# Minus the biased attention score and its minimum from one VectorE operation per branch, with the score scale moved into the key norm's weights

## The chip, the cores and the metric

The kernel runs on one core of a Trainium2 chip. The metric is the device time of one execution in microseconds (us). Three runs of the kernel before took 1355.65, 1356.13 and 1357.22 us; the median is 1356.13 us.

## What is computed

The reference is a trunk of two decoder layers over 256 tokens of width 1024. Each layer projects the normed input once, feeds three groups of heads (a state space model, a convolution module and a sparse attention), adds them through an output projection, and goes on with cross attention and a feed-forward part (dense in layer 0, the best two of eight experts in layer 1). The change lies in the sparse attention, of which these lines matter:

```
q = rms_norm(q, q_gain)                                  # 8 query heads of 64
k_slc = rms_norm(k_s, k_gain[1]);  k_win = rms_norm(k_w, k_gain[2])   # 2 key heads each
scale = HEAD_DIM ** -0.5
s_s = einsum(q, k_slc) * scale + bias_s                  # bias: table[bucket(distance)], masked where the key is later
s_w = einsum(q, k_win) * scale + bias_w
p = exp(s - max(s)) / sum(exp(s - max(s)))               # per row, for each branch by itself
o = gate_s * (p_s @ v_s) + gate_w * (p_w @ v_w) + gate_c * (compressed branch)
```

With 256 tokens every block is selected and the window covers all keys, so the selected and the window branch (below: b = 0 and b = 1) have the same bias and the same mask and differ in their keys and values.

## The kernel before

The 256 queries are two blocks (i = 0, 1) of 128 rows, which lie on the 128 partitions. Block 0 sees 128 keys, block 1 sees 256 (nk). A loop of 16 steps v runs over block and head, v = 8 i + n, in each layer; the code of each engine has this loop and its order is written out by hand. Every engine works through its own queue in order and waits on semaphores. The counter u is 20 l + v.

What each engine does at step v:

- TensorE, function scores(p), line 1837: one product for both branches of a head, into PSUM bank 0 (even v) or 1 (odd v), for the pair of heads v = 2p and 2p + 1. scores(p) is issued at the end of step v = 2p - 3, after the transposes and values of that step. The second bank of a pair may be written when VectorE has drained step 2p - 1, so the scores run one pair ahead of the softmax. banks.open is that wait.
- VectorE, lines 1330 to 1340: waits for the product and for the s_of buffer, forms scale times score plus bias of both branches in one operation (line 1337, 128 x 2 nk elements, PSUM and SBUF into SBUF) and adds one to the bank's drain semaphore; it waits for that itself, then takes the negated row maximum of both branches in one operation (line 1340) and adds one to max_ready. M holds the bias rows, read backwards.
- ScalarE, function probs, line 577: waits for max_ready, then one exponential per branch with the row maximum as its bias and the row sum as a second output (the read of the accumulator is a record of its own). After the second it adds one to probs_ready. Then it copies the transposed probabilities of step v - 1 out of PSUM (pt_copy, line 585).
- TensorE: waits for probs_ready, transposes the probabilities (line 1902), and multiplies those of step v - 1 with the values (function values, line 1572).

Other work is placed between these steps: on VectorE after step 1 the inner part of the compression, the centring of the convolution's layer norm and the gate of the state space model (lines 1191 to 1215), after step 2 the sums of the compressed keys (lines 1090, 1224), after step 5 and 13 the scores of the compressed branch (lines 1275 to 1282), after step 6 gate_halves (line 1295), after step 9 combine (lines 1300 to 1312) and the gain of the convolution's norm (line 1257), after step 10 conv_silu (line 1264). On TensorE fillers (line 1924, products that nobody reads) stand ahead of scores(p).

gk holds the products of the query and key gains, one column per layer and branch; it is made once at the start (lines 1115 to 1120). Its columns 1 and 2 multiply the keys of the two branches when they are copied to kT (line 1185), column 0 multiplies the compressed keys, whose scores are scaled by themselves at line 1275.

Of the kernel before, what the change touches and what calls it, by code (L numbers as in the profile page):

```python
# [19 lines left out]
ALU = mybir.AluOpType  # L20
ACT = mybir.ActivationFunctionType
AX = mybir.AxisListType.X

P = 128
# [18 lines left out]
SCALE = HD ** -0.5  # L43
# [199 lines left out]
def trunk(nc, x, mem, w_in, w_small, w_x, w_out, t5_table, ffn_w, router, moe_w, par_cols, s5_lam, s5_bc,  # L243
          consts, t5_hot, bias_rows, out):
    with ExitStack() as ctx:
        sem = Sems(nc, ctx)
        banks = Banks(sem)
# [10 lines left out]
        def ps(name):  # L258
            return pb[banks.bank(name)]
# [9 lines left out]
        M = late[0][:, 0:NH * FX].rearrange("p (h x) -> p h x", h=NH)  # L269
        par = sb("par", [P, 268])  # L270
        gk = sb("gk", [P, L, 4])
# [34 lines left out]
        nmx = sb("nmx", [P, 4, 2])  # L306
        sums = sb("sums", [P, NT, 2, NH])
# [47 lines left out]
        s_of = [scr[:, 0], scr[:, 1], spare[:, 0], spare[:, 1]]  # L355
        pt_of = [scr[:, 2], scr[:, 3], spare[:, 2], spare[:, 3]]

        def at(v): return (v + 2) % 4
# [13 lines left out]
        G_TAPS, G_HEAD = P, P + 64 * L  # L372
# [15 lines left out]
        for l in range(L):  # L388
# [3 lines left out]
            for c in range(CH if l == 0 else 0):  # L392
                s = FF_SLOTS[c]
# [125 lines left out]
        def _(act):  # L519
# [55 lines left out]
            def probs(buf, b, src, scale, to, m):  # L575

                return act.activation(s_of[buf][:, b * src.shape[-1]:(b + 1) * src.shape[-1]], src, ACT.Exp,  # L577
                                      bias=nmx[:, m, b:b + 1], scale=scale, accum_out=to)
# [12 lines left out]
            for l in range(L):  # L591
# [142 lines left out]
                for v in range(2 * NH + 1):  # L734
# [2 lines left out]
                    nk = P * (i + 1)  # L737
                    u = 20 * l + v
                    if v < 2 * NH:
                        act.wait_ge(sem["max_ready"], u + 1)  # L740
                        for b in range(2):
                            e = probs(at(v), b, s_of[at(v)][:, b * nk:b * nk + nk], 1.0, sums[:, i, b, hh:hh + 1], at(v))
                        e.then_inc(sem["probs_ready"], 1)
                    if v == 1:
                        cmp_tanh()
# [196 lines left out]
        def _(dve):  # L942
            n_own = [0]

            def own(i):
                n_own[0] += 1
                i.then_inc(sem["dve_step"], 1)
                dve.wait_ge(sem["dve_step"], n_own[0])
# [149 lines left out]
            for l in range(L):  # L1098
# [12 lines left out]
                if l == 0:  # L1111
                    for make in (weights, s5_turns(0)):
                        for _ in make:
                            pass
                    for m in range(L):
                        for b in range(3):
                            own(dve.tensor_tensor(gk[:, m, b:b + 1], par[:, G_HEAD + m:G_HEAD + m + 1],
                                                  par[:, G_HEAD + 2 + 3 * m + b:G_HEAD + 3 + 3 * m + b], ALU.mult))
                        own(dve.tensor_tensor(gk[:, m, 3:4], par[:, G_HEAD + 8 + m:G_HEAD + 9 + m],
                                              par[:, G_HEAD + 10 + m:G_HEAD + 11 + m], ALU.mult))  # L1120

# [202 lines left out]
                for v in range(2 * NH):  # L1324
                    i, n = divmod(v, NH)
                    hh = HEADS[n]
                    nk = P * (i + 1)
                    u = 20 * l + v
                    nm = f"sc{i}{n}_{l}"
                    banks.wait(dve, nm)  # L1330
                    if v >= 4:
                        banks.wait(dve, transposed(u - 4))
                    elif u >= 2 and v < 2:
                        banks.wait(dve, transposed(u - 2))
                    bias = M[:, hh, P:P * i + 256][:, ::-1].unsqueeze(1).to_broadcast([P, 2, nk])
                    S = s_of[at(v)][:, 0:2 * nk].rearrange("p (b s) -> p b s", b=2)
                    dve.scalar_tensor_tensor(S, ps(nm)[:, 0:2 * nk].rearrange("p (b s) -> p b s", b=2), SCALE, bias,
                                             ALU.mult, ALU.add).then_inc(banks.drain(nm), 1)
                    dve.wait_ge(banks.drain(nm), banks.count(nm, None, False) + 1)
                    dve.tensor_reduce(nmx[:, at(v)], S, AX, ALU.max, negate=True).then_inc(sem["max_ready"], 1)  # L1340
                    if v == 1:
                        cmp_inner()
                        ln_center()
                        glu_out()
                        cmp_gated()
                    if v == 2:
                        cmp_sums()
                    if v == 3:
                        cmp_keys()
                    if v == 4:  # L1350
                        cmp_keys_in()
                    if v == 5:
                        ln_scale()
                    if v == 6:
                        gate_halves()
                    if v in C_EXPS:
                        c_scores(C_EXPS.index(v))
                    if v in C_SUMS:
                        c_sums(C_SUMS.index(v))
                    if v == COMBINE:  # L1360
                        combine(0)
                    if v == CONV_GAIN:
                        conv_gained()
                    if v == CONV_SILU:
                        conv_silu()
                    if v == Y_SCALE:
                        y_scale(0)
# [879 lines left out]
```

## Time and profile before

| | us |
|---|---|
| median of three runs | 1356.13 |
| lowest, highest run | 1355.65, 1357.22 |
| span of the profiled execution, first to last instruction | 1354.2 |
| the same execution's time outside the span | not recorded; median less span is 1.9 |
| TensorE busy in the span | 1301.9 |
| VectorE busy in the span | 636.3 |
| ScalarE busy in the span | 424.7 |
| line 1337, 32 operations | 17.6 |
| line 1340, 32 operations | 17.7 |

The attention loop of layer 0 lies at 98 to 150 us of the span and that of layer 1 at 548 to 601 us. Times in the rows below count from the start of the span. In the timeline rows a group "x4" is four instructions of one kind that follow each other; for TensorE the first number is the start of the first of them and the second the time from there to the modelled end of the last. A bracket gives the idle time of that engine ahead of the row and what ended it. Layer 1's loop shows the same pattern as layer 0's, 449.8 us later at its start and 451.0 us later at its end.

### The profile page before, as it was taken

The numbers are of one execution on the slowest core, as the hardware profiler recorded it, in microseconds if no ns is written. First come the engines' busy times: TensorE is split into PE (matmuls) and PEld (weight loads), VectorE is DVE, ScalarE is ACT, GpSimd is POOL, SyncE is SP. The second block draws the span as 40 slices with busy tenths as digits, with TensorE's granted clock in tenths as the row PEclk, the third lists the DMA queues.
The fourth block names the chain that finished last, engine by engine and source line by source line (L and its number), as shares of the span: only waits on it lengthen the run. The fifth ranks groups of instructions, "written<-read, shape, count | busy, mean of one in ns | idle before, by whom it ended". The sixth has DMA issues, their size and how long they took to land.

```text
span 1354.2 us, 48384 instructions
## 1 busy us (share of the span) xinstructions
PE 1301.9 (96%) x21480; PEld 1076.0 (79%) x21480; DVE 636.3 (47%) x1404; ACT 424.7 (31%) x847; POOL 89.6 (7%) x139
## 2 busy tenths in 40 slices
PE   6999898999999999989889999999999999999998
PEld 5756555777777685654679999999999999999997
DVE  7877313013321246751345555555545555555554
ACT  4426313001002131541323334343343433334342
POOL 0350100000000027000000000000000000000000
PEclk8999999999999999989999999999999999999999
DMA  8530044224331154102669999999999999999990
GB/s 353 216 124 3 1 186 191 92 106 186 152 128 62 69 208 156 64 1 99 274 225 423 426 426 427 426 426 426 427 426 426 427 425 428 425 426 426 426 391 33
DMA packets 32865, 357.68 MB, mean 264 GB/s; under 512 B 3715, under 2 KB 5379, under 8 KB 6700
## 3 DMA queue, kind: packets, MB, share of 16 engines
q1 hardware_dynamic: 30656, 353.78, 63.2%
q10 hardware_dynamic: 2156, 3.18, 0.7%
q8 instruction: 35, 0.57, 0.2%
q14 instruction: 18, 0.15, 0.0%
HBM read 355.88 MB, written 1.06 MB: 264 GB/s over the span
## 4 chain that ended last, share of the span: by engine, by line
PE 89%; DVE 5%; ACT 2%; issue 2%; POOL 1%; DMA 1%; POOLq 0%; DVEq 0%; SPq 0%; ACTq 0%
PE bank L2109 29%; PE bank L1564 27%; PE bank L2125 14%; PE bank L2056 6%; PE bank L2171 2%; PE bank L1572 2%; PE bank L2096 2%; PE bank L1837 1%; PE bank L1714 1%; PE bank L1584 1%; PE bank L1902 1%; PE bank L1924 1%; DVE ring L970 1%; ACT ring L536 1%; PE bank L1658 1%
## 5 line engine op out<-in xcount | busy, mean ns | idle before, releaser
L2109 PE MATMUL bank<-R,ring 128*64 128x80 f32 x11264 | 421.7, 233 | 0.7 <-DVEq L952 0.7
L2109 PEld LDWEIGHTS bank<-R,ring 128*64 128x64 f32 x11264 | 403.0, 137 | 8.3 <-issue 8.3
L1564 PE MATMUL bank<-ring 128*128 128x256 f32 (+1 forms) x1408 | 366.2, 419 | 8.6 <-DVE ring L970 4.9
L1564 PEld LDWEIGHTS bank<-ring 128*128 128x128 f32 x1408 | 267.5, 191 | 106.3 <-issue 67.5
L843 ACT ACTIVATE ring<-ring 128x1024 f32<-128x1024 f32 x176 | 186.0, 1057 | 146.7 <-PE bank L2125 146.7
L2125 PE MATMUL bank<-zz,ring 128*64 128x80 f32 x5632 | 224.7, 233 | 0.0
L2125 PEld LDWEIGHTS bank<-zz,ring 128*64 128x64 f32 x5632 | 207.9, 137 | 0.0
L1526 DVE SCALAR_TENSOR_TENSOR zz<-zz,bank 128x80 f32<-128x80 f32 x176 | 41.9, 238 | 198.8 <-PE bank L2109 198.3
L1505 DVE COPY ring<-ring 128x1024 f32<-128x1024 f32 x177 | 121.6, 687 | 2.2 <-DVE R L1495 1.9
L1509 DVE COPY ring<-ring 128x1024 f32<-128x1024 f32 x177 | 121.7, 687 | 0.1
L839 ACT ACTIVATE X<-bank 128x80 f32<-128x80 f32 x176 | 41.7, 237 | 243.9 <-PE bank L2109 243.9
L1433 DVE SCALAR_TENSOR_TENSOR zz<-X,bank 128x256 f32<-128x256 f32 x22 | 9.3, 421 | 171.9 <-ACT X L829 171.9
L1521 DVE SCALAR_TENSOR_TENSOR zz<-X,bank 128x80 f32<-128x80 f32 x176 | 41.8, 237 | 85.3 <-ACT X L839 84.2
L2056 PE MATMUL bank<-ring,zz 128*128 128x512 f32 x176 | 79.0, 592 | 0.0
L829 ACT ACTIVATE X<-bank 128x256 f32<-128x256 f32 x22 | 8.4, 384 | 202.8 <-PE bank L1564 202.8
L2056 PEld LDWEIGHTS bank<-ring,zz 128*128 128x128 f32 x176 | 33.4, 190 | 33.1 <-issue 32.0
L1381 DVE TENSOR_TENSOR h<-h,bank 128x512 f32<-128x512 f32 x20 | 13.8, 688 | 60.3 <-PE bank L1564 56.8
L536 ACT ACTIVATE ring<-h 128x1024 bf16<-128x1024 f32 x12 | 12.7, 1057 | 81.0 <-DVE h L1381 79.5
L577 ACT ACTIVATE ring<-ring,nmx 128x128 f32<-128x128 f32 (+1 forms) x64 | 28.4, 444 | 15.6 <-DVE nmx L1340 15.6
L2171 PE MATMUL bank<-R 80*128 80x512 f32 x64 | 29.6, 605 | 2.0 <-ACT R L848 2.0
L1584 PE MATMUL bank<-cst,xn 128*128 128x128 f32 x128 | 20.8, 293 | 8.5 <-DVE ring L970 3.8
L1564 PE MATMUL bank<-ring,R 128*128 128x256 f32 (+1 forms) x96 | 28.7, 452 | 0.0
(299 smaller groups left out, 1026.6 us busy)
## 6 DMA issues: line engine op xcount, KB each, us to landing
ring<-moe_w_dram SPq DMA_DIRECT2D x177, 1536.0 KB, 11.1
ring<-ffn_w_dram SPq DMA_DIRECT2D x11, 3072.0 KB, 10.0
ring<-w_in_dram SPq DMA_DIRECT2D x6, 2048.0 KB, 10.5
ring<-w_out_dram SPq DMA_DIRECT2D x4, 2048.0 KB, 8.7
ring<-w_x_dram SPq DMA_DIRECT2D x2, 3072.0 KB, 10.5
ring<-w_small_dram SPq DMA_DIRECT2D x2, 2896.0 KB, 9.8
ring<-w_in_dram SPq DMA_DIRECT2D x2, 2144.0 KB, 21.0
ring<-bias_rows_dram ACTq DMA_DIRECT2D x1, 1536.0 KB, 10.5
```

What stands on the lines that cost most here:

```text
L839: act.activation(eth, pb[0][:, 0:CAP], ACT.Tanh, scale=0.5).then_inc(sem["e_tanh"], 1)
L843: act.activation(st_down, hs[:, HS_ORDER[t % NHS], 2048:3072], ACT.Copy).then_inc(sem["down_staged"], 1)
L1505: dve.tensor_copy(st_gate, hs[:, HS_ORDER[t % NHS], 0:1024]).then_inc(sem["gate_staged"], 1)
L1509: dve.tensor_copy(st_value, hs[:, HS_ORDER[t % NHS], 1024:2048]).then_inc(sem["value_staged"], 1)
L1521: dve.scalar_tensor_tensor(es[t % 2], eth, 1.0, pb[0][:, 0:CAP], ALU.add, ALU.mult).then_inc(sem["e_half"], 1)
L1526: dve.scalar_tensor_tensor(eT, es[t % 2], 0.5, pb[1][:, 0:CAP], ALU.mult, ALU.mult).then_inc(sem["e_gated"], 1)
L1564: i = pe.matmul(out_ap, a, b, start=(k == 0), stop=(k == n - 1))
L1584: e = pe.transpose(ps(nm)[:, 256 * k + P * i:256 * k + P * i + P], src[:, i, P * (2 * g + k):P * (2 * g + k) + P], ident)
L2056: e = pe.matmul(pb[4 + g][:], hT[:, t % 2, P * (g // 2):P * (g // 2) + P], w[:, mt, 512 * (g % 2):512 * (g % 2) + 512], start=(t == 0), st ...
L2109: e = pe.matmul(pb[out_bank][c0:c0 + 64, 0:CAP], half[:, P * k + c0:P * k + c0 + 64], xg[:, k], start=(k == 0), stop=(k == KT - 1), tile_p ...
L2125: e = pe.matmul(o[c0:c0 + 64], st_down[:, P * b + c0:P * b + c0 + 64], eT, start=False, stop=last, tile_position=(0, c0), skip_group_check ...
L2171: done(nm, pe.matmul(ps(nm)[:], ogT[:, P * (g // 2):P * (g // 2) + P], ye[:, 512 * (g % 2):512 * (g % 2) + 512], start=True, stop=True))
```

## The change

The scale moves into columns 1 and 2 of gk, so that the products of queries and keys come out scaled. For each branch VectorE then runs one tensor_tensor_reduce on its nk columns: it writes minus (score + bias) and in the same operation the row minimum of that, which is minus the row maximum. The exponential takes its input with scale -1. The operation of branch 0 signals max_ready, that of branch 1 the bank's drain; ScalarE waits for the one before the exponential of branch 0 and for the other before that of branch 1. VectorE no longer waits for itself between two operations.

```diff
                     if v < 2 * NH:
-                        act.wait_ge(sem["max_ready"], u + 1)
+                        nm = f"sc{i}{n}_{l}"
                         for b in range(2):
-                            e = probs(at(v), b, s_of[at(v)][:, b * nk:b * nk + nk], 1.0, sums[:, i, b, hh:hh + 1], at(v))
+                            if b:
+                                act.wait_ge(banks.drain(nm), banks.count(nm, None, False) + 1)
+                            else:
+                                act.wait_ge(sem["max_ready"], u + 1)
+                            e = probs(at(v), b, s_of[at(v)][:, b * nk:b * nk + nk], -1.0, sums[:, i, b, hh:hh + 1], at(v))
                         e.then_inc(sem["probs_ready"], 1)
...
                         for b in range(3):
-                            own(dve.tensor_tensor(gk[:, m, b:b + 1], par[:, G_HEAD + m:G_HEAD + m + 1],
-                                                  par[:, G_HEAD + 2 + 3 * m + b:G_HEAD + 3 + 3 * m + b], ALU.mult))
+                            own(dve.scalar_tensor_tensor(gk[:, m, b:b + 1], par[:, G_HEAD + m:G_HEAD + m + 1], SCALE if b else 1.0,
+                                                         par[:, G_HEAD + 2 + 3 * m + b:G_HEAD + 3 + 3 * m + b], ALU.mult, ALU.mult))
...
-                    bias = M[:, hh, P:P * i + 256][:, ::-1].unsqueeze(1).to_broadcast([P, 2, nk])
-                    S = s_of[at(v)][:, 0:2 * nk].rearrange("p (b s) -> p b s", b=2)
-                    dve.scalar_tensor_tensor(S, ps(nm)[:, 0:2 * nk].rearrange("p (b s) -> p b s", b=2), SCALE, bias,
-                                             ALU.mult, ALU.add).then_inc(banks.drain(nm), 1)
-                    dve.wait_ge(banks.drain(nm), banks.count(nm, None, False) + 1)
-                    dve.tensor_reduce(nmx[:, at(v)], S, AX, ALU.max, negate=True).then_inc(sem["max_ready"], 1)
+                    bias = M[:, hh, P:P * i + 256][:, ::-1]
+                    for b in range(2):
+                        dve.tensor_tensor_reduce(s_of[at(v)][:, b * nk:b * nk + nk], ps(nm)[:, b * nk:b * nk + nk], bias, -1.0, 3e38,
+                                                 ALU.add, ALU.min, nmx[:, at(v), b:b + 1])\
+                           .then_inc(banks.drain(nm) if b else sem["max_ready"], 1)
```

## Rows read from the trace of the kernel before

**Rows 1.** Page, part 4: the chain that ended last, by engine
```profile
PE 89%; DVE 5%; ACT 2%; issue 2%; POOL 1%; DMA 1%; POOLq 0%; DVEq 0%; SPq 0%; ACTq 0%
```

**Rows 2.** Windows (columns: busy us and instructions by engine, granted clock, DMA), layer 1's loop
```profile
545.00:600.00 55.00, 50.45 (x536) 34.30 (x536) 34.12 (x86) 32.88 (x113) 2.99 (x7) 0.94 0.09 37
```

**Rows 3.** Groups of VectorE by line and shape, 98 to 150 us
```profile
L1340 DVE TENSOR_REDUCE nmx<-ring 128x2 f32<-128x512 f32 x8 | 5.5, 686 | 0.3
L1337 DVE SCALAR_TENSOR_TENSOR ring<-bank,ring 128x512 f32<-128x512 f32 x8 | 5.5, 684 | 0.4 <-DVE ring L1257 0.3
...
L1337 DVE SCALAR_TENSOR_TENSOR ring<-bank,ring 128x256 f32<-128x256 f32 x8 | 3.3, 416 | 2.1 <-PE bank L1837 1.8 <-issue 0.2
...
L1275 DVE SCALAR_TENSOR_TENSOR pc<-bank,ring 128x60 f32<-128x60 f32 x4 | 0.9, 250 | 7.1 <-PE bank L1572 7.1
...
L1191 DVE COPY cb<-bank 128x1 f32<-128x1 f32 x1 | 0.1, 149 | 0.0
```

**Rows 4.** Timeline (start, us, engine, line), steps 10 and 11 and scores(6)
```profile
127.45 0.69 DVE L1337 SCALAR_TENSOR_TENSOR ring<-bank,ring 128x512 f32<-128x512 f32 x1 [0.34 <-DVE ring L1257]
128.18 0.69 DVE L1340 TENSOR_REDUCE nmx<-ring 128x2 f32<-128x512 f32 x1
...
128.78 0.68 DVE L1264 SCALAR_TENSOR_TENSOR ring<-R,ring 128x512 f32<-128x512 f32 x1
...
129.38 0.68 DVE L1337 SCALAR_TENSOR_TENSOR ring<-bank,ring 128x512 f32<-128x512 f32 x1
...
130.12 1.12 PE L1837 MATMUL bank<-ring 64*128 64x512 f32 x2 [0.80 <-DVE ring L1337]
```

**Rows 5.** Timeline, ScalarE: an operation without accumulator read, then two exponentials
```profile
119.36 0.49 ACT L772 ACTIVATE R<-memT,par 128x256 f32<-128x256 f32 x1
119.76 0.49 ACT L577 ACTIVATE ring<-ring,nmx 128x256 f32<-128x256 f32 x1
...
120.25 0.49 ACT L577 ACTIVATE ring<-ring,nmx 128x256 f32<-128x256 f32 x1
```

**Rows 6.** Timeline, step 3 and scores(2), and scores(3) for comparison
```profile
106.96 0.40 DVE L1337 SCALAR_TENSOR_TENSOR ring<-bank,ring 128x256 f32<-128x256 f32 x1
107.01 1.10 PE L1837 MATMUL bank<-ring 64*128 64x256 f32 x4
...
110.77 0.70 PE L1837 MATMUL bank<-ring 64*128 64x256 f32 x4
```

**Rows 7.** Timeline, steps 6 and 7 on VectorE, ahead of scores(4)
```profile
114.45 0.42 DVE L1337 SCALAR_TENSOR_TENSOR ring<-bank,ring 128x256 f32<-128x256 f32 x1 [0.19 <-issue]
...
115.25 0.18 DVE L1295 TENSOR_SCALAR gates<-gates 128x48 f32<-128x48 f32 x1
...
115.46 0.42 DVE L1337 SCALAR_TENSOR_TENSOR ring<-bank,ring 128x256 f32<-128x256 f32 x1
...
115.94 0.29 PEld L1837 LDWEIGHTS bank<-ring 64*128 64x128 f32 x2 [0.71 <-DVE ring L1337]
```

**Rows 8.** Timeline, step 14 from its scores to its transposes
```profile
140.71 0.68 DVE L1337 SCALAR_TENSOR_TENSOR ring<-bank,ring 128x512 f32<-128x512 f32 x1
...
141.43 0.69 DVE L1340 TENSOR_REDUCE nmx<-ring 128x2 f32<-128x512 f32 x1
...
142.15 0.51 ACT L577 ACTIVATE ring<-ring,nmx 128x256 f32<-128x256 f32 x1 [1.02 <-DVE nmx L1340]
...
143.29 0.76 PE L1902 MATMUL bank<-cst,ring 128*128 128x128 f32 x4 [2.51 <-ACT ring L577]
```

**Rows 9.** Windows over the same 30 products, layers 0 and 1; one of the router
```profile
131.17:134.21 3.04, 3.04 (x30) 2.55 (x30) 2.18 (x4) 1.29 (x5) 0.00 (x0) 1.00 0.00 0
580.75:585.25 4.50, 4.50 (x30) 3.67 (x30) 2.15 (x4) 1.30 (x5) 0.00 (x0) 0.63 0.02 4
...
694.00:695.00 1.00, 0.88 (x3) 0.16 (x1) 0.96 (x6) 0.00 (x0) 0.00 (x0) 0.50 1.01 430
```

**Rows 10.** Timeline, TensorE ahead of the last window of group 9
```profile
691.06 1.25 PE L1564 MATMUL bank<-R,memT 128*128 128x8 f32 x10 [1.46 <-DVE R L1450]
```

## The prediction

> **What bounds the kernel now.** I read the chain that ended last first. It is TensorE's for 89% and VectorE's for 5% [rows 1], so a faster VectorE operation is worth nothing by itself: only where TensorE stands still for it. Next the windows. In layer 1's attention loop TensorE is busy for 50.45 of 55 us, VectorE for 34.12, and the granted clock is 0.94 [rows 2]; some 4.5 us a layer is all that waiting can give back, plus what the clock costs. Then the timeline of the loop, step by step, for every place where TensorE stands idle behind lines 1337 or 1340. There are four, alike in both layers:
>
> - S2: scores(2) starts at 107.01, but its second bank is freed only when step 3's line 1337 ends (106.96 + 0.40 = 107.36). Its four products take 1.10 us where scores(3) takes 0.70 [rows 6]. Stall 0.40.
> - S4: scores(4)'s second bank waits for steps 6 and 7 on VectorE, 114.45 to 115.88 [rows 7].
> - S6: scores(6)'s second bank waits for steps 10 and 11, with conv_silu between, 127.45 to 130.06 [rows 4].
> - S14: the transposes of step 14 wait for its exponentials, and these for both VectorE operations; TensorE is idle for 2.51 us [rows 8].
>
> Everywhere else in the loop TensorE reaches VectorE's result late, and a gain there ends as VectorE's idle time.
>
> **The price of an operation.** Two numbers matter for each: its duration, and its pitch, the time until the next one on VectorE starts when nothing holds that. A 128x512 operation shows 0.69 us, but the reduce at 128.18 is followed at 128.78: pitch 0.60, 0.09 under its duration. Line 1337 at 127.45 is followed at 128.18 by the reduce that waits for it: 0.73 [rows 4]. So a pair now costs VectorE 0.73 + 0.60 = 1.33 us in block 1. In block 0 steps 6 to gate_halves take 115.25 - 114.45 = 0.80 [rows 7].
>
> The new operation isn't in the trace. Its shape is half of line 1337's with the same sources. In block 1 that is 128x256 from PSUM and SBUF: 0.416, taken as 0.42 [rows 3]. In block 0 it is 128x128: between 0.25 for 60 columns and 0.42 for 256; line 1337's own slope is (684 - 416) / 256 = 1.05 ns a column, so 0.416 - 128 x 1.05 ns = 0.28; I take 0.29 [rows 3]. Less 0.08 the pitches are 0.34 and 0.21.
>
> The second output is the unknown. I call its extra k, for the pitch as for the completion, per operation. Below zero it can't be: the same columns are read and more is written. The nearest row of a second output is ScalarE's: line 772 without one has pitch 119.76 - 119.36 = 0.40, the exponential of the same size with one 120.25 - 119.76 = 0.49 [rows 5]: k = 0.09. The smallest VectorE operation takes 0.149 [rows 3]; appended with the usual overlap it adds 0.149 - 0.08 = 0.07, and if it must wait for the main one to end, 0.149 + 0.03 = 0.18. I take 0.07, the row of the same engine, near ScalarE's 0.09, and keep 0 and 0.18 for the range.
>
> The Trainium skill ("VectorE: DVE Perf Modes", section "Two Vector instructions with no wait between them") says an operation that also writes out its accumulator is two instructions, the second one the read. The trace shows that for ScalarE only. Its rule for authors on the same page, to minimize the number of operations and not the semaphores, speaks against this change, which makes two operations and two reads out of two; against it stands that the columns streamed per head fall from 4 nk to 2 nk.
>
> **Part by part.** One head, with the new pair a, b:
>
> - VectorE pitch of the pair: block 0 2 x (0.21 + 0.07) = 0.56, was 0.80; block 1 2 x (0.34 + 0.07) = 0.82, was 1.33.
> - Bank drained after the start: block 0 0.28 + 0.29 + 0.07 = 0.64, was 0.42; block 1 0.41 + 0.42 + 0.07 = 0.90, was 0.69. This is later, by 0.2 us, and scores(p) waits for it, with the transposes queued behind on TensorE.
> - First exponential may start: block 0 0.29 + 0.07 + 0.03 = 0.39, was 0.88; block 1 0.52, was 142.15 - 140.71 = 1.44 [rows 8].
> - The added wait on ScalarE ahead of the second exponential. Queued behind it are pt_copy and, through probs_ready, TensorE's transposes. Operation b of block 1 is done 0.90 after the start, the second exponential wouldn't start before 0.52 + 0.49 = 1.01: cost nothing. Up to k of about 0.16 it stays so; at 0.18 it is some 0.03.
> - gk: six one-column operations at the start become six others of one column. Nothing, within 6 x 0.05 either way; the row of such a size is 0.149 [rows 3]. The scale on kT costs nothing, since line 1185 multiplies by gk anyway. No DMA and no queue is moved.
>
> The places:
>
> - S2: ScalarE's step 2 is at least 0.49 earlier, and the squares, sums (lines 1090, 1224) and step 3 that follow it too. Step 3 then starts by 106.47 and its bank is drained by 107.11, before TensorE has issued the first bank (107.01 + 0.32). The stall of 0.40 is gone, 0.39 counted. Next late is scores(2) itself. With the full k of 0.18 it still holds within 0.05.
> - S4: now 1.43. After: 0.56 + gate_halves 0.21 [rows 7] + 0.64 = 1.41. Gain 0.02; in k, 1.43 - (1.13 + 4k).
> - S6: now 2.61. After: 0.82 + conv_silu 0.60 [rows 4] + 0.90 = 2.32. Gain 0.29; in k, 2.61 - (2.04 + 4k).
> - S14: 1.44 - 0.52 = 0.92 earlier; in k, 0.99 - k. Then the pipeline of exponentials, copies and products is TensorE's and ScalarE's, and everything up to the output projection moves with it. Next late is TensorE's own work of step 13.
>
> Sum per layer 0.39 + 0.02 + 0.29 + 0.92 = 1.62, or 2.25 - 9k. Two layers: 3.2 us (k = 0: 4.5; k = 0.18: 1.3). What follows each loop is a serial chain through TensorE [rows 1], with no transfer waited for in the loop (DMA share 0.09 [rows 2]), so the gain reaches the end. The sum stands against the span of 1354.2: it becomes 1351.0. Median and span differ by 1.9, of which I know nothing better; on the median of 1356.13 the change makes 1352.9.
>
> **The clock.** Three times in the two loops the granted clock is at its lower level, 1.2 GHz instead of 2.4, for a few us: behind S14 in both layers and behind S6 in layer 1 only. The same 30 products take 3.04 us at 1.00 and 4.50 at 0.63 [rows 9]: such a stretch costs 1.5 us. Ahead of the two at S14 TensorE was idle for 2.51 us [rows 8]; that becomes 1.6. Ahead of the stretch at the router it was idle for 1.46 us only [rows 10, 9], so the shorter gap may well still bring it. That S6 brought one in layer 1 and none in layer 0, from the same idle times, says that this isn't settled by the gap alone. My forecast keeps three.
>
> **Rivals.**
>
> - Fewer stretches: the gaps at S14 no longer lower the clock, once or twice. 1352.9 - 1.5 = 1351.4, or 1349.9. For it: the gap shrinks by more than a third. Against: the 1.46 us at the router.
> - The read waits: k = 0.18. Gain 1.3 us, 1354.8. For it: the second output needs the last column of the first. Against: ScalarE's 0.09.
> - A new stretch: S6 lowers the clock in layer 0 as well, where nothing but the phase kept it up. 1352.9 + 1.5 = 1354.4.
> - Slower: the bank is freed later. S4 and S6 hold two pairs each, and every k costs them 4k, S14 k: the gain turns at k = 0.25. Were the new operation to stream at half rate (0.42 and 0.69 instead of 0.29 and 0.42), S2 gives 0.39, S14 0.48, S4 -0.50 and S6 -0.79: 0.42 lost a layer, 1357.0. With k = 0.40 from a program that starts slowly it is 1.35 a layer and 1358.8. For it: nothing in the trace shows this kind of operation. Against: all VectorE rows of one size lie within 0.01 us, whatever the operation [rows 3].
>
> The Trainium skill ("Vector Engine (DVE) Microarchitecture Reference", section 7, "Points that are easy to get wrong") has a rule that would halve the rate: a scalar_tensor_tensor with two SBUF sources that aren't bf16, as no port is left for the accumulator. Here one source is in PSUM, so by that rule the full rate stands; no row tests it.
>
> **How the numbers follow.** Forecast as summed, three stretches: 35%, 1352.9. Fewer stretches: 28%. Read waits: 17%. New stretch: 10%. Slower: 10%. The range goes from 1348.8 (k near 0 with two stretches gone, 1348.6, is nearly the end of what the cases hold) to 1356.0, leaving out most of the slower case. A difference of 0.2%, 2.7 us, is about what a measurement of this kernel can tell from none. The bound lies at 1353.4, close above my forecast: of its 35% some 26 are faster, with the 28% of fewer stretches and a few from the others 58%. Slower takes the higher end of the slower case, 8%. Same 34%.
>
> **What would show it.** VectorE: new rows of 0.29 and 0.42 with a read whose pitch is k; pair pitches of 0.56 and 0.82. TensorE: scores(2) at 0.70 instead of 1.10; scores(4)'s second bank where it was, scores(6)'s 0.3 earlier after conv_gained; idle of 1.6 us ahead of step 14's transposes; both loops 1.6 us shorter, windows elsewhere unchanged. Windows of the clock: a count of stretches other than three moves the time by 1.5 each. Wrong would be a k above 0.15, a second exponential that waits for the drain, or a stall that appears at scores(3), (5) or (7).

## The result, and the profile after

| | before | after |
|---|---|---|
| median of five runs each, us | 1355.65 | 1349.58 |
| lowest, highest, us | 1354.07, 1357.22 | 1346.66, 1351.57 |
| ratio after / before, 95% interval | | 0.9947, 0.9929 to 0.9964 |
| profiled execution: time, span, us | span 1354.2 | 1346.66, 1344.8 |
| mean granted clock of that execution | 0.992 | 0.997 |

The three runs that stand ahead of the prediction are among the five of before. The change is faster by 6.1 us by the medians and by 7.2 us by the ratio, half a per cent, and the interval leaves 1 out. The forecast was 3.2 us (1352.9); the time lies in the range of 1348.8 to 1356.0, but the gain is about twice the one forecast. The profiled execution of after is the fastest of its five, and its span is 9.4 us shorter than that of before.

The first view of after is two lines of the page: busy time by engine, and the chain that ended last, by engine (it answers to [rows 1]). The third is the window over layer 1's loop that answers to [rows 2], 55 us that begin 2.98 us ahead of scores(0) in both kernels.

```profile
PE 1295.0 (96%) x21480; PEld 1070.7 (80%) x21480; DVE 621.9 (46%) x1468; ACT 424.4 (32%) x847; POOL 89.6 (7%) x139
...
PE 88%; DVE 6%; ACT 3%; issue 2%; POOL 1%; DMA 1%; POOLq 0%; DVEq 0%; SPq 0%; ACTq 0%
...
539.30:594.30 55.00, 51.96 (x560) 34.98 (x561) 29.82 (x123) 32.77 (x113) 2.98 (x7) 0.97 0.09 36
```

VectorE is busy for 14 us less than before and TensorE is the bound as it was. In 55 us of layer 1 TensorE now works for 51.96 us instead of 50.45, VectorE for 29.82 instead of 34.12, and the granted clock is 0.97 instead of 0.94.

The new operations, as groups of VectorE by line and shape over 98 to 148 us. The last two columns are busy time with the mean ns of one, and the idle time ahead. They answer to [rows 3].

```profile
L1341 DVE CUSTOM_DVE_ANT_0 ring<-bank,ring 128x256 f32<-128x256 f32 x16 | 5.9, 421 | 0.9 <-PE bank L1840 0.5 <-DVE ring L1261 0.4
L1341 DVE CUSTOM_DVE_ANT_0 ring<-bank,ring 128x128 f32<-128x128 f32 x13 | 3.3, 284 | 0.8 <-PE bank L1840 0.5 <-issue 0.3
...
L1341 DVE DVE_READ_ACCUMULATOR2_ANT nmx<- 128x1 f32 x29 | 2.4, 82 | 0.0
```

The trace gives the fused operation under the name CUSTOM_DVE_ANT_0. Its durations are those of the forecast, 0.42 and 0.28 us (0.42 and 0.29 there). The second output is a record of its own, 82 ns. What it costs is seen in the timeline only (start, us, engine, line). Here are steps 10 and 11 with scores(6), which answer to [rows 4]:

```profile
124.77 0.42 DVE L1341 CUSTOM_DVE_ANT_0 ring<-bank,ring 128x256 f32<-128x256 f32 x1 [0.38 <-DVE ring L1261]
125.12 0.08 DVE L1341 DVE_READ_ACCUMULATOR2_ANT nmx<- 128x1 f32 x1
125.12 0.42 DVE L1341 CUSTOM_DVE_ANT_0 ring<-bank,ring 128x256 f32<-128x256 f32 x1
125.47 0.08 DVE L1341 DVE_READ_ACCUMULATOR2_ANT nmx<- 128x1 f32 x1
125.47 0.69 DVE L1268 SCALAR_TENSOR_TENSOR ring<-R,ring 128x512 f32<-128x512 f32 x1
126.07 0.41 DVE L1341 CUSTOM_DVE_ANT_0 ring<-bank,ring 128x256 f32<-128x256 f32 x1
...
126.41 0.42 DVE L1341 CUSTOM_DVE_ANT_0 ring<-bank,ring 128x256 f32<-128x256 f32 x1
...
126.89 1.12 PE L1840 MATMUL bank<-ring 64*128 64x512 f32 x2 [0.17 <-DVE nmx L1341]
```

The read of the accumulator starts at the same time as the next operation (125.12, 125.12; 125.47, 125.47). The pitch of one operation is 0.35 us, its duration less the usual overlap of some 0.07 us: k is 0. From the start of step 10 to the second bank of scores(6) it is 126.89 - 124.77 = 2.12 us, where before it was 130.12 - 127.45 = 2.67.

Step 14, which answers to [rows 8]:

```profile
137.48 0.42 DVE L1341 CUSTOM_DVE_ANT_0 ring<-bank,ring 128x256 f32<-128x256 f32 x1
...
137.82 0.42 DVE L1341 CUSTOM_DVE_ANT_0 ring<-bank,ring 128x256 f32<-128x256 f32 x1
137.94 0.51 ACT L577 ACTIVATE ring<-ring,nmx 128x256 f32<-128x256 f32 x1
...
138.45 0.49 ACT L577 ACTIVATE ring<-ring,nmx 128x256 f32<-128x256 f32 x1
...
139.09 0.66 PE L1905 MATMUL bank<-cst,ring 128*128 128x128 f32 x4 [1.52 <-ACT ring L577]
```

The first exponential starts 0.46 us after the step instead of 1.44, the second follows it without a wait for the drain, and TensorE is idle for 1.52 us instead of 2.51. For scores(2), [rows 6], and scores(4), [rows 7], the timeline of TensorE reads, after in the first two lines and scores(4) of before in the third:

```profile
105.25 0.70 PE L1840 MATMUL bank<-ring 64*128 64x256 f32 x4
...
112.64 1.71 PE L1840 MATMUL bank<-ring 64*128 64x512 f32 x4
...
114.94 2.13 PE L1837 MATMUL bank<-ring 64*128 64x512 f32 x4
```

scores(2) takes 0.70 us where it took 1.10; scores(4) takes 1.71 where it took 2.13.

**The account.** I measured each loop from the start of scores(0) to the start of the second combine (line 1307, after: 1311), and the distances between fixed places inside it.

| us | layer 0 | layer 1 |
|---|---|---|
| loop before | 98.08 to 149.71: 51.63 | 547.98 to 600.70: 52.72 |
| loop after | 96.42 to 143.96: 47.54 | 542.28 to 591.30: 49.02 |
| gained at S2 | 0.39 | 0.39 |
| S4 | 0.55 | 0.28 |
| S6 | 0.55 | 0.54 |
| S14 | 0.98 | 0.99 |
| earlier places | 0.06 | 0 |
| stretch at the lower clock gone, net | 1.54 | 1.47 |

A stretch at the lower clock is a few us in which the granted clock is 0.50, that is 1.2 GHz. This window of before lies in the one behind step 14 of layer 0:

```profile
144.00:145.00 1.00, 1.00 (x17) 0.92 (x16) 0.93 (x5) 1.00 (x5) 0.00 (x0) 0.50 0.00 0
```

So 2.5 and 2.2 us a layer, 4.7 in all, come from the steps, and 3.0 from the granted clock inside the loops. 1.7 us more of the 9.4 lie ahead of the first loop: scores(0) starts at 98.08 in before and at 96.42 in after. That part can't be put down to the change: in four more executions it starts at 97.90 and 97.07 (before) and at 97.98 and 97.17 (after), with the same work ahead of it. Between the loops, and from the second loop to the end, the two profiles take the same time within 0.1 us. The runs' medians differ by less than the two spans, since the profiled run of after had the highest clock of its five, 0.997; the other four had 0.993 to 0.994.

### The profile page after: what moved, and what is told of

It reads as the page before. It is cut to its first block, busy times and chain, and to the rows that moved or that the text cites. A ratio compares the mean times of both kernels' runs of the same rounds, so it can differ in the third digit from the quotient of the medians.

```text
span 1344.8 us, 48448 instructions
## 1 busy us (share of the span) xinstructions
PE 1295.0 (96%) x21480; PEld 1070.7 (80%) x21480; DVE 621.9 (46%) x1468; ACT 424.4 (32%) x847; POOL 89.6 (7%) x139
## 4 chain that ended last, share of the span: by engine, by line
PE 88%; DVE 6%; ACT 3%; issue 2%; POOL 1%; DMA 1%; POOLq 0%; DVEq 0%; SPq 0%; ACTq 0%
PE bank L2112 29%; PE bank L1567 25%; PE bank L2128 14%; PE bank L2059 6%; PE bank L2174 2%; PE bank L1575 2%; PE bank L2099 2%; PE bank L1840 1%; PE bank L1717 1%; PE bank L1927 1%; PE bank L1905 1%; DVE ring L974 1%; PE bank L1587 1%; ACT ring L536 1%; PE bank L1661 1%
```

## Experiments

In all texts below "before" and "after" are the two kernels. The shared runs of before have a median of 1356.41 us (23 runs) beside the kernels with fillers and with the compressed scores moved (e1, e2, e6, e7) and of 1356.62 us (17 runs) beside the other four edits; both sets go from 1354.1 or 1354.3 to 1361.0. Where a kernel is set against after, the runs of the two were made at different times, and the median of before moved by up to 1.0 us between such times. A loop's length without low-clock stretches is its length when it has none, or less 1.5 us for each that it has: before 50.1 and 49.7 us, after 47.5 and 47.5.

### One small operation more behind each new one (e3_small_op)

```diff
+        dum = sb("dum", [P, 16])
...
                                                  ALU.add, ALU.min, nmx[:, at(v), b:b + 1])\
                            .then_inc(banks.drain(nm) if b else sem["max_ready"], 1)
+                        own(dve.tensor_tensor(dum[:], cst[:, 0:16], cst[:, 16:32], ALU.mult))
```

> The changed kernel with one small VectorE operation (128x16, waited for, some 0.21 us of pitch) behind each new operation, so 0.42 us more a head and the bank drained 0.21 us later after the step starts. Theory A (VectorE counts only where TensorE waits for a freed bank): S4 and S6, which each hold one whole pair and the first part of a second, grow by 3 x 0.21 = 0.63 us; S2 by 0 (step 3 still drains its bank before scores(2) has issued its first); S14 by 0.05 (the second exponential now waits for the drain). 1.3 us a layer, 2.6 in all: 1352.2 on the median of 1349.6; the loops without a low-clock stretch 48.8 us long instead of 47.5. Rival B (VectorE's rate is what sets the loop): 16 x 0.42 = 6.7 us a layer, 1363. Rival C (S4 and S6 were not shortened by VectorE): 0, 1349.6. A low-clock stretch more or less moves each by 1.5.

Measured: 1353.56 us, ratio 0.998 (0.9963 to 0.9998), so 4.0 above after. Without stretches the loops take 49.3 and 49.4 us, 1.8 and 1.9 more than after. TensorE's timeline at scores(4) and scores(6):

```profile
113.94 2.19 PE L1842 MATMUL bank<-ring 64*128 64x512 f32 x4
...
127.59 1.12 PE L1842 MATMUL bank<-ring 64*128 64x512 f32 x2 [0.89 <-DVE nmx L1342]
129.30 1.12 PE L1842 MATMUL bank<-ring 64*128 64x512 f32 x2 [0.59 <-DVE nmx L1342]
```

S4 grew by 0.48 (2.19 for 1.71) and by 0.16 ahead of its first bank, S6 by 0.21 + 0.42 = 0.63, S2 by 0.18 and S14 by 0.06. 0.24 came at a place that I hadn't listed, the values of step 1, which wait for VectorE's centring (idle 0.50 instead of 0.26). VectorE was given some 6.4 us a layer (32 operations at a pitch of 0.20) and the loop grew by 1.8: B falls, and C as well. It is theory A, whose 1.3 us a layer were 0.5 short, with two terms of 0.2 that it had at 0.

### Both operations waited for before the first exponential (e4_wait_both)

```diff
                             else:
                                 act.wait_ge(sem["max_ready"], u + 1)
+                                act.wait_ge(banks.drain(nm), banks.count(nm, None, False) + 1)
```

> The changed kernel, but ScalarE waits for both of VectorE's operations before the first exponential. Theory A (S14 is gained because the first exponential starts behind half of the work): the first exponential of step 14 starts 0.34 us later after the step's start (0.80 instead of 0.46) and TensorE's idle time ahead of the transposes grows from 1.52 to 1.86; S2, S4 and S6 as in the changed kernel, since the bank is drained at the same time. 0.3 us a layer, 0.7 in all, 1350.3; to be read in the timeline. Rival B (the second exponential is what TensorE waits for, and it was held up by VectorE anyway): idle time stays 1.5. Rival C (all of S14 is from the early start): the idle time returns to 2.5.

Measured: 1352.15 us in its one run. Step 14 on ScalarE and TensorE, and two windows behind it (columns as in [rows 2], the granted clock is the third number from the end):

```profile
141.46 0.51 ACT L577 ACTIVATE ring<-ring,nmx 128x256 f32<-128x256 f32 x1 [0.45 <-DVE nmx L1342]
...
142.60 0.44 PE L1906 MATMUL bank<-cst,ring 128*128 128x128 f32 x2 [1.93 <-ACT ring L577]
...
144.00:145.00 1.00, 1.00 (x10) 0.69 (x9) 0.43 (x2) 0.49 (x2) 0.00 (x0) 0.50 0.00 0
145.00:146.00 1.00, 1.00 (x7) 0.75 (x6) 0.00 (x0) 0.59 (x1) 0.00 (x0) 0.50 0.00 0
```

The exponential starts 0.87 us after the step (140.59) and TensorE is idle for 1.93 us; 1.86 was expected, B would have 1.5 and C 2.5. So of the 0.99 us of S14 0.41 is the split by branch and 0.58 is the fusing. S6 is as in after (0.68 and 0.17). What no theory had said: layer 0 has a stretch at 1.2 GHz behind step 14 again, where after has none, and another at S6; layer 1 has one behind step 14, as after does. With a single run the medians say little, but the two profiles can be set side by side: this span is 5.6 us longer than after's, of which 0.8 is idle time at step 14, 3.1 the two stretches more, and 1.6 the later start of the first loop (97.97 for 96.42), which moves between executions of one kernel as well.

### The operations taken apart again (e5_split_unfused)

```diff
-                        dve.tensor_tensor_reduce(s_of[at(v)][:, b * nk:b * nk + nk], ps(nm)[:, b * nk:b * nk + nk], bias, -1.0, 3e38,
-                                                 ALU.add, ALU.min, nmx[:, at(v), b:b + 1])\
+                        S = s_of[at(v)][:, b * nk:b * nk + nk]
+                        dve.tensor_tensor(S, ps(nm)[:, b * nk:b * nk + nk], bias, ALU.add).then_inc(sem["half"], 1)
+                        dve.wait_ge(sem["half"], 2 * (16 * l + v) + b + 1)
+                        dve.tensor_reduce(nmx[:, at(v), b:b + 1], S, AX, ALU.max, negate=True)\
```

> The changed kernel with each branch's operation taken apart again: an addition, a wait for it, and a reduce for the negated maximum; the scale in the gains and the order by branch stay. Theory A (the gain is from fusing; the split by branch alone loses): per step of block 1 VectorE takes 2 x (0.45 + 0.34) = 1.58 us of pitch instead of 0.69 and the bank's signal comes at 1.66 us instead of 0.77; in block 0 1.04 instead of 0.42 and 1.10 instead of 0.49. S6 becomes 1.58 + 0.60 + 1.66 = 3.8 us (before 2.61, after 2.06), S4 1.04 + 0.21 + 1.10 = 2.35 (before 1.43, after 1.1), S14's second exponential waits for the drain at 1.69 (before: 1.93, after 0.95). Against the changed kernel + 1.8 + 1.2 + 0.7 and S2 0.4: 4.1 us a layer, 8.2 in all, 1357.8, slower than the kernel before by some 2. Rival B (the early first exponential is the gain): S14 keeps its 0.99 us, 1352 at most.

Measured: 1365.72 us, ratio 1.007 (1.0045 to 1.0095): 9.1 above its before and 16.1 above after, where 2 and 8.2 were expected. TensorE at scores(6) and at step 14:

```profile
130.11 1.12 PE L1842 MATMUL bank<-ring 64*128 64x512 f32 x2 [1.53 <-DVE nmx L1344]
132.28 2.07 PE L1842 MATMUL bank<-ring 64*128 64x512 f32 x2 [1.05 <-DVE nmx L1344]
...
148.06 0.66 PE L1907 MATMUL bank<-cst,ring 128*128 128x128 f32 x4 [2.28 <-ACT ring L577]
```

S6 has 1.73 us more idle time than after (1.8 expected), S14 0.76 (0.7), and S4 grew by 1.24 (1.2). S2 grew by 0.96 where 0.4 was expected. Two more came unlisted: 0.59 at the values of step 1, and in layer 0 0.32 at scores(3), which got no stall in after. The lengths without stretches are 53.1 and 52.9 us, 5.5 a layer over after: 11.0 us. The other 5 go with the clock, which is read from profiles alone: this kernel has five low stretches in its loops (131 to 139 twice, 148 to 153, 589 to 593, 602 to 606), after has one to two. A's direction stands; its size was short by 1.4 a layer and by the clock. The fusing is what pays; the split by branch without it loses.

### Fillers ahead of step 14's transposes (e1_fill_after, e2_fill_before)

The same edit on after (2 fillers) and on before (4); the index of the list is v // 2:

```diff
-FILLERS = [4, 2, 2, 2, 5, 2]
+FILLERS = [4, 2, 2, 2, 5, 2, 2]
...
-                    if v % 2 or not 2 <= v < 2 * NH - 2:
+                    if v % 2 or not 2 <= v < 2 * NH:
...
-                    if v % 2 and v + 3 < 2 * NH:
+                    if v % 2 and v + 1 < 2 * NH:
```

> The changed kernel with two more filler products on TensorE ahead of step 14's transposes, in the gap in which it waits for ScalarE (1.52 us in the changed kernel's profile). Theory A (the steps give 4.7 us, the rest of the measured 6.1 is fewer stretches at 1.2 GHz behind that gap): no stretch is left behind step 14, the profile shows granted clock 1.00 there in both layers, and the time is 1 to 1.5 us under the changed kernel's, 7 to 7.5 under the kernel before. Theory B (all 6.1 us come from steps, the clock's stretches are as frequent as before): 6.1 under the kernel before or a little less for the fillers.

> The kernel before with four fillers in the same gap, which is 2.51 us long there; they need 2.2. VectorE's and ScalarE's work is untouched. Theory A: both stretches at 1.2 GHz behind step 14 go, worth 1.5 us each, so up to 3.0 us under the kernel before (2.5 to 3.0 where not every execution had both). Theory B: no difference beyond 0.5 us.

Measured: on after 1350.0 us, ratio 0.9944 (0.9923 to 0.9964), no different from after itself. On before 1357.0 us, ratio 0.9989 (0.9975 to 1.0003). Step 14 and a window behind it, in the kernel made from before:

```profile
143.14 0.66 PE L1902 MATMUL bank<-cst,ring 128*128 128x128 f32 x4 [0.58 <-ACT ring L577]
...
144.00:145.00 1.00, 1.00 (x20) 0.86 (x17) 0.96 (x4) 1.00 (x5) 0.00 (x0) 1.00 0.00 0
```

The transposes wait as long as before for ScalarE, but TensorE is idle for 0.58 us only, and the clock stays at 2.4 GHz behind it in both layers. Layer 0's loop is 50.07 us long, 1.56 shorter than before's, with the same work on VectorE and ScalarE: the gap does lower the clock there. Yet the run as a whole doesn't gain: of theory A's time, the 2.5 to 3.0 us on before didn't come, nor did the 1 to 1.5 us under after (1350.0 beside 1349.6). Five of the twelve runs made from before took 1352.9 to 1354.9 us, the others 1356.9 to 1358.2, and the profile is of the slowest. It has two stretches in a row at layer 1's S6 (580 to 587) where before has one, one more at 218 to 222, and one idle gap of TensorE among the experts' products that none of the other profiles has:

```profile
704.59 1.33 PE L2109 MATMUL bank<-R,ring 128*64 128x80 f32 x32 [2.09 <-issue]
```

The kernel from after has lost the stretch that after has behind step 14 in layer 1 (idle 0.47 instead of 1.53), but it has one at S6 in both layers where after has none. It also takes 2.1 us more at the router, where it has three stretches in a row and after has one. Neither is shown to be the fillers' doing: unedited executions have them as well (the two in a row at S6 in r2, one at S6 in each layer and the three at the router in r1, below). So the fillers show what the gap at step 14 does, and not that filling it makes the kernel faster.

### Compressed scores of block 1 behind step 14 (e6_cscores_late_before, e7_cscores_late_after)

What is late at S14 is VectorE, since the four compressed-score operations stand ahead of step 14's. One edit on each kernel puts them behind:

```diff
-C_SCORES, C_EXPS, C_TURN, C_SUMS, C_VALUES = (4, 12), (5, 13), (6, 14), (7, 15), (8, 15)
+C_SCORES, C_EXPS, C_TURN, C_SUMS, C_VALUES = (4, 12), (5, 14), (6, 14), (7, 15), (8, 15)
```

> The kernel before with the compressed branch's scores of block 1 (lines 1275 to 1282 and their exponential) placed behind step 14's two VectorE operations and not ahead of them. Theory A: TensorE's wait of 2.51 us ahead of step 14's transposes nearly goes (to 0 to 0.3), 2.2 to 2.5 us a layer, 4.4 to 5.0 us in all, and the stretches behind it with it, so 5 to 8 us under the kernel before. If the wait were in truth for something else (ScalarE's order, the scores themselves), under 1 us.

> The changed kernel with the same move. Theory A: its wait of 1.52 us there goes, 3 us in two layers, and the remaining stretches: 3 to 4.5 us under the changed kernel. Against the kernel before with the same move only places S2, S4 and S6 are left, 0.39 + 0.3 to 0.55 + 0.55 us a layer: 2.5 to 3.0 us less than it. If the fused operation had a general worth beyond the four places, the difference to that kernel would stay near 4.7 to 6.

Measured: on before 1350.91 us, ratio 0.9961 (0.9946 to 0.9977); on after 1345.78, ratio 0.9915 (0.9896 to 0.9934). The first fence is the kernel from before, the second the one from after: transposes of steps 14 and 15, and between them the exponential of step 15.

```profile
138.99 0.66 PE L1902 MATMUL bank<-cst,ring 128*128 128x128 f32 x4
...
141.57 0.66 PE L1902 MATMUL bank<-cst,ring 128*128 128x128 f32 x4 [0.34 <-ACT ring L577]
...
140.43 0.51 ACT L577 ACTIVATE ring<-ring,nmx 128x256 f32<-128x256 f32 x1 [1.02 <-DVE nmx L1340]
```

```profile
139.57 0.66 PE L1905 MATMUL bank<-cst,ring 128*128 128x128 f32 x4
...
141.65 0.60 PE L1905 MATMUL bank<-cst,ring 128*128 128x128 f32 x4
```

Step 14 waits in neither. In the kernel from before step 15 now waits for VectorE, which has the compressed scores ahead of its slow pair; in the one from after it doesn't. The loops without stretches are 48.3 and 47.9 us against 45.9 and 45.95: the moved work leaves the change worth some 2.2 us a layer, where the expectation had 1.2 to 1.5. It takes S14 away as a place of gain and gives a smaller one at step 15 and behind it, 0.8 us a layer. The two medians lie 5.1 us apart, which is what the expectation had for a worth beyond the four places. In the loops that worth is the 0.8 at step 15: the two profiles show 4.3 us of steps in all. The rest is not traced; the runs made from before are spread over 8 us (1347.3 to 1355.5). The version from after beats both kernels.

### Two more pieces moved out from between the pairs (e8_later_copies)

```diff
-C_SCORES, C_EXPS, C_TURN, C_SUMS, C_VALUES = (4, 12), (5, 13), (6, 14), (7, 15), (8, 15)
+C_SCORES, C_EXPS, C_TURN, C_SUMS, C_VALUES = (4, 12), (7, 14), (7, 14), (7, 15), (8, 15)
...
-                    if v == 6:
+                    if v == 7:
...
-                    if v == CONV_SILU:
+                    if v == CONV_SILU + 1:
```

> The changed kernel with the compressed scores of block 1 behind step 14's two operations, as in the experiment of that name before, and besides: gate_halves and ScalarE's and VectorE's compressed work of block 0 behind step 7 instead of step 6 or 5, and conv_silu behind step 11 instead of step 10, so that neither stands between the pairs that free the second bank of scores(4) and of scores(6). Theory A (these operations add their pitch to S4 and S6): against the kernel with the compressed scores alone moved (1345.8) S6 gives 0.60 us a layer, if TensorE's idle time there allows, of which the trace shows 0.17 ahead of the second bank and 0.68 ahead of the first, and S4 0.2; 0.8 to 1.6 in all, 1344.2 to 1345.0. Rival B (what is moved is late at its new place: conv_silu holds up step 12, the compressed values TensorE): no gain or a loss, 1345.8 to 1347.

Measured: 1341.47 us, ratio 0.9886 (0.9867 to 0.9906), the fastest of all. TensorE at scores(6):

```profile
125.91 1.81 PE L1840 MATMUL bank<-ring 64*128 64x512 f32 x4 [0.68 <-DVE nmx L1341]
```

Both banks are now issued in one go; the transposes behind follow after 1.74 us, in after it was 127.95 - 125.61 = 2.34. S6 gave the 0.60 expected, S4 0.4 where 0.2 was. What was moved held nothing up at its new place, so B falls. The loops are 44.95 us long in both layers, without one low stretch: 1.0 shorter than in the kernel with the compressed scores alone moved. That makes 2.0 of the 4.3 us between the medians; the mean clock of the runs went from 0.993 to 0.996.

### Both kernels again, for where their stretches lie (r1 to r4)

No edit: the kernel after in r1_after_look and r3_after_look, the kernel before in r2_before_look and r4_before_look.

> The changed kernel once more, for a second profile of it. Open is where its low-clock stretches lie from one execution to the next. Theory A (the idle time ahead of step 14's transposes decides; 1.52 us brings a stretch now and then): 0 or 1 stretch in two loops behind step 14, 0 to 2 behind S6; the loops without stretches stay 47.5 us. Rival B (chance decides everywhere alike, the gap doesn't matter): as many stretches behind step 14 as the kernel before has. Rival C (the places are fixed for a given program): the same single stretch, behind step 14 of layer 1, and 49.0 us for that loop.

> The kernel before once more, for a second profile of it. Theory A (2.5 us of idle TensorE ahead of step 14's transposes always lowers the clock): a stretch behind step 14 in both layers, one or none behind S6 in each; the loops without stretches stay 50 us. Rival B (chance alike everywhere): fewer than two behind step 14. Rival C (fixed places): S14 of both layers and S6 of layer 1, and the two stretches at 14 to 21 us again.

> The changed kernel, a third profile. Expected as in the second: by theory A at most one of its two step 14s with a stretch, and S6 with 0 to 2; by rival B two; by rival C just layer 1's step 14.

> The kernel before, a third profile. By theory A both step 14s with a stretch again; by rival B not always; by rival C all five stretches where the first profile has them.

Measured, with the first profile of each:

| | time, us | loops, us | low stretches: S6 | S14 |
|---|---|---|---|---|
| before | span 1354.2 | 51.63, 52.72 | 0, 1 | 1, 1 |
| r2 | 1356.56 | 51.63, 54.52 | 0, 2 in a row | 1, 1 |
| r4 | 1354.59 | 52.84, 52.40 | 0, 0 | 2 in a row, 2 in a row |
| after | 1346.66 | 47.54, 49.02 | 0, 0 | 0, 1 |
| r1 | 1351.48 | 49.08, 49.04 | 1, 1 | 0, 0 |
| r3 | 1348.89 | 48.92, 49.11 | 0, 1 | 1, 0 |

One more run of before, made beside these four, took 1361.21 us.

The first fence is r4 at step 14 of layer 1, the second r1 at the same place: TensorE, and a window behind it.

```profile
593.04 1.11 PE L1902 MATMUL bank<-cst,ring 128*128 128x128 f32 x4 [2.51 <-ACT ring L577]
...
594.00:595.00 1.00, 1.00 (x17) 0.92 (x16) 0.96 (x5) 0.93 (x3) 0.00 (x0) 0.50 0.00 0
```

```profile
589.54 0.66 PE L1905 MATMUL bank<-cst,ring 128*128 128x128 f32 x4 [1.53 <-ACT ring L577]
...
590.00:591.00 1.00, 1.00 (x21) 0.78 (x20) 0.93 (x5) 1.00 (x5) 0.00 (x0) 1.00 0.00 0
```

Rival C falls at once: the places change from one execution to the next. B doesn't fit: behind 2.51 us of idle time the clock fell in six loops of six, behind 1.52 in two of six, though six loops are few. Theory A stands for step 14, though r3 and the first profile of after show that 1.52 us does bring a stretch at times; the two in a row at S6 in r2 are one more than it had. The two loops together take 105.2 us on the mean of the three profiles of before, with 3.7 stretches, and 97.6 on that of after, with 1.7: 7.7 us less, of which 4.7 are the steps' and 3.0 the clock's.

Outside the loops the six profiles settle the rest. On the mean of three, the first loop starts 0.5 us earlier in after (97.2 for 97.7 us), the part between the loops takes 398.3 us in all six, and the part behind the second loop takes 1.4 us more in after (754.0 for 752.7), over half of it from r1, with its three stretches in a row at the router. That makes 7.7 + 0.5 - 1.4 = 6.8 us between the mean spans, 1353.9 and 1347.1.

## Why the prediction was half right

**The places: right.** All four gained, and the loops show no other of over 0.1 us in after. The added wait of ScalarE for the drain cost nothing, as said. scores(3), (5) and (7) got no new stall. The experiment with a small operation added shows where the account had no reserve: S2 and the values of step 1 were each within 0.2 us of a wait.

**k: the term that was mis-sized.** The forecast took 0.07 us per operation from VectorE's smallest operation with the usual overlap. The row has 0.08 us for the read, but it starts with the next operation and adds 0 to the pitch, and the reader of the result doesn't wait for more than the operation: the exponential starts 0.46 us after the step, 0.42 + 0.04. With 9k a layer and two layers that is 1.3 us. The formula at k = 0 gives 4.5; the steps gave 4.7. ScalarE's read, the nearest row of a second output, does add 0.09 to the pitch [rows 5]; the two engines differ, and the row of another engine drew the estimate the wrong way.

**By place.** S2 0.39 forecast, 0.39 measured. S14 0.92 and 0.99 (0.99 - k). S6 0.29 and 0.54: 4k and nothing else (0.57 at k = 0). S4 0.02 and 0.55 or 0.28: 0.30 is the formula at k = 0, which is what layer 1 shows. In layer 0 there was a gap of 0.19 us put down to issue ahead of step 6 in [rows 7] which after doesn't have there; I had left it out as not the change's. That is the 0.2 over the formula.

**The clock: the step that failed.** The forecast kept three stretches, with the argument that the router's stretch came behind 1.46 us of idle time, so a gap of 1.6 might still bring one. The forecast gave the clock nothing; it gave back 3.0 us, two stretches, in the loops. At step 14 the idle time sorts the loops of all profiles. 2.51 us (before, three profiles): clock down to 1.2 GHz in six of six. 2.28 (operations apart) and 1.93 (both waited for): four of four. 1.52 to 1.59 (after, three profiles, and the small operation): two of eight. 0.58 and 0.47 (fillers): none of four. No wait (compressed scores late): none of six. So the change makes the stretch at this place an accident where it had been sure. The row at the router, one stretch behind 1.46 us, was read too strongly: it said that a gap of 1.6 can bring one, not that it does. Nor does that gap by itself account for it: the clock falls at the router in all fourteen profiles, in r2 at 689.3, ahead of the gap and of the products behind it.

At S6 the idle time doesn't sort them: 0.68 and 0.17 us had a stretch in seven of twelve loops (after, with fillers, both waited for, compressed scores late), 0.56 and 0.80 in three of ten. With 0.89 and 0.59 it was one of two, with 1.53 and 1.05 two of two, and with 0.68 alone none of two. It comes in one layer, in the other, in both or in none, whatever the kernel, so "behind S6 in layer 1 only" was one draw and no property of the kernel; "three stretches" likewise was the count of one execution. What decides at S6 is open.

The forecast that the evidence bore out is the sum at k = 0 with two stretches fewer, 4.5 + 3.0 = 7.5 us, and the loops of three profiles each give 7.7. The rival of fewer stretches, at 28%, had this mechanism; its 1349.9, 0.3 from the median, came with k = 0.07 in its sum and with nothing for the parts outside the loops, so that it is so near is luck. The runs' 6.1 to 7.2 us stay up to 1.6 below 7.7, and so do the mean spans, 6.8 apart. That difference lies outside the loops, where the executions of one and the same kernel differ by as much: the start of the first loop by 1.6 us and the part behind the second by 1.7 in the three profiles of after. The same 16 products ahead of the first loop take 4.07 us in r1 and 2.18 in the first profile of after. What decides that is open, and so is the gap of 2.09 us in the kernel with fillers made from before.

**The rivals that fell.** Read waits (k = 0.18), slower (turn at k = 0.25) and half rate (0.69 us for 256 columns): the rows have 0, and 0.42. A new stretch at S6 in layer 0 came in r1 and in three edited kernels with after's idle times, but in both other profiles of after it didn't, and on the whole stretches went.

**The rule weighed.** The Trainium skill ("VectorE: DVE Perf Modes", section "Two Vector instructions with no wait between them") has it that an operation with an accumulator output is two instructions, and the trace agrees: 29 reads of 82 ns. The same page's rule to minimize the number of operations (section "Rules for kernel authors") would have counted four against two and spoken against the change. Here the pitch decided: two operations of half the columns with reads that add nothing take 2 x 0.35 us, two operations over both branches took 1.33.

## What to carry to other kernels

Where an engine is not the bound, list the few places where the bound engine waits for it and price the change there in pitch and completion, not in busy time: 14 us less of VectorE were 4.7 us of time. Put other work behind the operations that free a buffer or release a chain, not between or ahead of them: on top of the fusing, moving such work shortened the two loops by 5.1 us without stretches (47.5 to 44.95 each), where the fusing had given 4.7, and the time by 8.1. When a gap on TensorE of some 2 us shrinks, count the stretch at the lower clock behind it as a likely part of the gain, but not as a sure one (the fillers removed it at step 14, and the median didn't move), and look at several profiles of the same kernel before taking its stretches for its own.

## What the runs showed of the hardware

- The read of VectorE's accumulator takes 0.08 us and starts together with the next operation; it adds nothing to the pitch, 0.35 us for 128x256 and 0.21 us for 128x128.
- A fused sum and minimum from PSUM and SBUF with a row result runs at the rate of a plain addition of that shape: 0.42 us for 128x256, as line 1342's addition in the kernel with the operations apart.
- Of one place, step 14: 1.93 us and more of idle TensorE were followed by a stretch at 1.2 GHz in ten loops of ten, 1.52 to 1.59 us in two of eight, under 0.6 in none of four. A single stretch at 1.2 GHz cost 1.5 us of the loop, two in a row that began inside the idle time 2.7.
- Neither the number of such stretches nor their places are a property of the kernel: three executions of one kernel had three, four and four of them in the two loops (before), and one, two and two (after).
